# mLSTM heads with the output gate's copy ahead of the strip sums and the denominators behind the next scores; the fourth output unit in a place of its own

## The reference, cut to what matters

```
proj = xn @ w_in                       # q, k (conv + silu), v, o_pre, gates
# each of 8 heads, L x L with causal mask:
dmat = b[t] - b[s] + ig[s];  w_intra = exp(dmat - m_t)
sm   = w_intra * (q @ k.T)             # q, k: 64 wide
num  = sm @ v                          # v: 128 wide
den  = sum(sm, axis=-1)
h    = num / max(abs(den), exp(-m_t))
h    = h * rsqrt(mean(h * h) + eps) * head_gain
out  = (h * sigmoid(o_pre)) @ w_out
# attention, last lines:  o @ w_out, 8 heads of 128
```

## Time and profile before

| | |
|---|---|
| Median of three runs | 2618.55 us |
| Profiled execution, its own time | 2618.54 us |
| Its span | 2616.8 us |
| TensorE matmul busy | 2484.6 us, 95% |
| VectorE busy | 1505.2 us, 58% |
| ScalarE busy | 500.7 us, 19% |
| POOL busy | 1668.6 us, 64% |
| Convolutions and values | about 1940 to 2024 us |
| mLSTM heads | about 2018 to 2197 us |

### The profile page before, as it was taken

How to read it: one execution, slowest core, us unless ns; L and a number is a source line. 1 busy time by engine, 2 the same in 40 slices (tenths; PEclk the granted TensorE clock), 3 DMA queues, 4 the chain that set the end, 5 groups by cost and what they waited for, 6 DMA issues and landing times.

```text
span 2616.8 us, 33925 instructions
## 1 busy us (share of the span) xinstructions
PE 2484.6 (95%) x11933; PEld 2010.5 (77%) x11933; DVE 1505.2 (58%) x1805; ACT 500.7 (19%) x969; POOL 1668.6 (64%) x716
## 2 busy tenths in 40 slices
PE   6998999999999998999999999999999998999998
PEld 4776776777878876888888878888887656887886
DVE  5867324686474467645444565534688667644456
ACT  4533222103000003111111220000131432100000
POOL 4425444577777776565556657877777214777774
PEclk8999999999999998999999999999999878999999
DMA  6212333422332322222222223322322101332331
GB/s 243 73 56 82 117 148 127 157 73 74 99 101 89 108 80 65 85 77 77 84 76 82 82 65 98 108 83 96 105 84 89 33 25 48 96 108 85 93 110 54
DMA packets 61728, 237.86 MB, mean 91 GB/s; under 512 B 7152, under 2 KB 12280, under 8 KB 58048
## 3 DMA queue, kind: packets, MB, share of 16 engines
q1 hardware_dynamic: 55008, 231.56, 26.7%
q10 hardware_dynamic: 6624, 5.03, 0.7%
HBM read 232.37 MB, written 2.10 MB: 90 GB/s over the span
## 4 chain that ended last, share of the span: by engine, by line
PE 81%; DVE 10%; ACT 3%; issue 2%; DVEq 1%; ACTq 1%; POOL 1%; DMA 1%; POOLq 0%
PE gg L575 18%; PE gg L576 18%; PE gg L577 18%; PE babcd L613 2%; PE babcd L614 2%; PE babcd L615 2%; PE gg L958 2%; PE gg L959 1%; PE gg L960 1%; PE babcd L575 1%; PE babcd L577 1%; PE babcd L576 1%; PE be L934 1%; PE babcd L943 1%; DVE tb L2016 1%
## 5 line engine op out<-in xcount | busy, mean ns | idle before, releaser
L475 POOL TENSOR_TENSOR w_hi<-raw,zero 128x1024 fp32r<-128x1024 f32 (+2 forms) x260 | 540.4, 2079 | 457.7 <-PE gg L577 345.4
L477 POOL TENSOR_TENSOR w_lo<-raw,w_hi 128x1024 fp32r<-128x1024 f32 (+2 forms) x260 | 696.2, 2678 | 37.0
L575 PE MATMUL gg<-h_hi,w_hi 128*128 128x512 f32 x1560 | 620.6, 398 | 13.0 <-DVE bf L2398 7.4
L576 PE MATMUL gg<-h_lo,w_hi 128*128 128x512 f32 x1560 | 614.2, 394 | 0.0
L577 PE MATMUL gg<-h_hi,w_lo 128*128 128x512 f32 x1560 | 613.9, 394 | 0.0
L575 PEld LDWEIGHTS gg<-h_hi,w_hi 128*128 128x128 f32 x1560 | 297.4, 191 | 83.5 <-DVE bf L2398 9.8
L577 PEld LDWEIGHTS gg<-h_hi,w_lo 128*128 128x128 f32 x1560 | 296.9, 190 | 63.3
L576 PEld LDWEIGHTS gg<-h_lo,w_hi 128*128 128x128 f32 x1560 | 297.7, 191 | 60.8
L466 POOL TENSOR_TENSOR w_hi<-raw,zero 128x1024 fp32r<-128x1024 f32 (+2 forms) x64 | 140.4, 2193 | 296.7 <-PE babcd L577 152.1
L2115 DVE TENSOR_TENSOR ta<-ff_s,gg 128x512 f32<-128x512 f32 x63 | 43.3, 688 | 320.6 <-PE gg L577 320.6
L575 PE MATMUL gg<-u_hi,w_hi 128*128 128x512 f32 x528 | 209.7, 397 | 4.2 <-issue 4.2
(11 more groups left out here) (623 smaller groups left out, 3960.5 us busy)
## 6 DMA issues: line engine op xcount, KB each, us to landing
raw<-in_w_ff_in_a SPq DMA_DIRECT2D x66, 512.0 KB, 3.5
raw<-in_w_ff_in_b SPq DMA_DIRECT2D x66, 512.0 KB, 3.5
raw<-in_w_att_qk SPq DMA_DIRECT2D x48, 512.0 KB, 3.5
raw<-in_w_ff_out_a SPq DMA_DIRECT2D x24, 704.0 KB, 4.1
raw<-in_w_ff_out_b SPq DMA_DIRECT2D x24, 704.0 KB, 4.1
late_raw<-in_w_ada SPq DMA_DIRECT2D x16, 1024.0 KB, 5.0
raw<-in_w_ml SPq DMA_DIRECT2D x25, 512.0 KB, 3.5
raw<-in_w_merge_a SPq DMA_DIRECT2D x16, 768.0 KB, 5.5
```

The source lines that it names most:

```text
L475: pool.tensor_tensor(hi, a, zero[:].to_broadcast([P, size * P]), ALU.add)
L477: pool.tensor_tensor(lo, a, hi, ALU.subtract).then_inc(S["units_split"], 1)
L575: pe.matmul(dst, w_hi[slot][:, blk], xs[0][:, k, :], start=k == 0, stop=False)
L576: pe.matmul(dst, w_hi[slot][:, blk], xs[1][:, k, :], start=False, stop=False)
```

## The change

In the heads, VectorE copies the output gate right after the products and sums the strips after that; `head_low` follows. TensorE does `head_sums(i-1)` after the first three score blocks of head i, and the scores and weights wait for four of the five `ml_sm` counts of the head before. ScalarE takes `head_deviation(i-1)` ahead of `denominator(i)`. In the convolutions `gate_rows` moves from behind conv(2) to behind conv(3), and `values_out(0)` from ahead of `conv_act(4)` to ahead of `conv_act(3)`. The fourth unit of `w_att_out` and `w_ml_out` is split into the last two tiles of `h_hi` and `h_lo`, free at that time, as soon as all units of the run before have been used.

```diff
+FOURTH = 6
...
+        w_hi.append(h_hi[:, 6:8, :].rearrange("p a b -> p (a b)"))
+        w_lo.append(h_lo[:, 6:8, :].rearrange("p a b -> p (a b)"))
...
-            def split_third(name, tenant, done):
-                u, w = FIRST[name] + 2, THIRD[name]
+            def split_apart(u, w, tenant, done):
                 pool.wait_ge(S[f"raw_landed{u % N_RAW}"], (u // N_RAW + 1) * 16)
                 pool.wait_ge(S[tenant], done)
-                a, hi, lo = raw[u % N_RAW][:, 0:KD * P], w_hi[w][:], w_lo[w][:]
+                a, hi, lo = raw[u % N_RAW][:, 0:KD * P], w_hi[w][:, 0:KD * P], w_lo[w][:, 0:KD * P]
...
                             elif name == "w_att_out":
-                                split_third(name, "att_scores", 14)
+                                split_apart(u0 + 2, THIRD[name], "att_scores", 14)
                             else:
-                                split_third(name, "ml_scores", 4)
+                                split_apart(u0 + 2, THIRD[name], "ml_scores", 4)
+                        elif s == 3 and name in ("w_att_out", "w_ml_out"):
+                            split_apart(u0 + 3, FOURTH, "units_used", u0)
...
-                        cols_mm(g[(u0 + s) % 2], (u0 + s) % 2, kb, xs, ...)
+                        slot = FOURTH if lead is not None and isinstance(i, int) else (u0 + s) % 2
+                        cols_mm(g[(u0 + s) % 2], slot, kb, xs, ...)
...   TensorE, head_scores(i)
-                wait(pe, "ml_sm", 5 * i)
+                wait(pe, "ml_sm", 5 * i - 1)
...
                 for j in (0, 1, 3):
                     block(j)
+                if i:
+                    head_sums(i - 1)
...
                 if i < 7:
                     head_rows(i + 1)
-                head_sums(i)
+            head_sums(7)
...   ScalarE
             for n in range(8):
-                if n == 4:
+                if n == 3:
                     wait(act, "rows_ready", 4)
...   head_weights(i)
-                wait(act, "ml_sm", 5 * i)
+                wait(act, "ml_sm", 5 * i - 1)
...
-                denominator(i)
                 if i:
                     head_deviation(i - 1)
+                denominator(i)
...   VectorE
-                if n == 2:
+                if n == 3:
                     gate_rows()
...   end of head_products(i)
                 v.drain()
+            def strip_sums():
                 own = lambda j: sm_t[:, ML_AT[j]:ML_AT[j] + SEQ - j * P]
                 tt(sm_sum[:], own(0)[:, P:SEQ], own(1), ALU.add)
...
                 head_products(i)
+                output_gate(i)
+                strip_sums()
                 if i > 2:
                     head_low(i - 3)
-                output_gate(i)
                 if i > 1:
                     head_norm(i - 2)
```

More of the change, by code:

```diff
@@ L538, in _ @@
                             if name in ("w_ff0_in_a", "w_att"):
-                                split_third(name, "units_used", u0)
+                                split_apart(u0 + 2, THIRD[name], "units_used", u0)
                             elif name == "w_att_out":
-                                split_third(name, "att_scores", 14)
+                                split_apart(u0 + 2, THIRD[name], "att_scores", 14)
                             else:
-                                split_third(name, "ml_scores", 4)
+                                split_apart(u0 + 2, THIRD[name], "ml_scores", 4)
+                        elif s == 3 and name in ("w_att_out", "w_ml_out"):
+                            split_apart(u0 + 3, FOURTH, "units_used", u0)
                         else:
@@ L680, in pair @@
                         wait(pe, "res_added", i * 2 + (nth * 8 + s - 1))
-                        cols_mm(g[(u0 + s) % 2], (u0 + s) % 2, kb, xs, **(first if isinstance(i, int) and s == 0 else {}))
+                        slot = FOURTH if lead is not None and isinstance(i, int) else (u0 + s) % 2
+                        cols_mm(g[(u0 + s) % 2], slot, kb, xs, **(first if isinstance(i, int) and s == 0 else {}))
                     if shift and isinstance(i, int):
```

## The result

The kernel after takes 2586.56 us, the median of four runs (2585.45 to 2593.54), against 2616.42 us for the kernel before on the same chip: a ratio of 0.989, interval 0.9865 to 0.9915. The profiled executions took 2618.54 (span 2616.8) and 2585.99 us (span 2584.2).

A forecast was written before the change was run, and what follows sets the result against it. TensorE was busy 95% of the span, so only its waits and slow-clock time could move the end. Terms -17.0 - 1.0 - 3.0 + 4.3 - 1.1 + 2.1 = -15.7 took 2618.55 to 2603 us; range 2594 to 2611, 8 in 10.

The forecast's parts named there:

- Heads 2 to 6: mLSTM heads: gate-copy waits of 9.7 us go and slow clock shrinks, 20.7 to 17.3 us each: -17.0, ends -9.7 and -22.
- First head: Head 1: the copy of gate 0 no longer stands behind sums that POOL held up: -1.0 us.
- Convolutions and values: Convolution stage: TensorE's waits of 2.7 and 1.3 us go, second-half values scaled earlier: -3.0, ends 0 and -4.
- Head 7's rows to the first w_ml_out matmul: Last mLSTM head: POOL's consecutive splits block three strip sums and later VectorE operations: +4.3 us, ends -3.1 and +6.
- Fourth w_ml_out unit: w_ml_out: the 4.2 us wait for POOL goes, but VectorE's read of unit 1 limits it: -1.1, ends 0 and -4.2.
- Last attention head: POOL's earlier fourth split blocks two of VectorE's small a_st operations, delaying scaling and transposes: +3.2 us.
- Fourth w_att_out unit: w_att_out: the same gain as for the fourth w_ml_out unit, -1.1 us.
- the short kind: Heads 2 to 6: without stops, most heads would keep only short 1.2 GHz stretches, giving 17.3 us per head.
- VectorE's own loop: Heads: VectorE's sequence of operations per head as the next bound, 16.3 us, behind the low end of -22.
- Rival (b): Heads: the clock stays up, VectorE's loop sets 16.3 us per head, the tail costs little: -25, 2594 us; chance 0.12.
- the strip sums, 4.7 us: Heads: strip sums start 0.9 us after the gate unit's end, POOL's w_hi and w_lo blocking the first and second.
- The denominator: ScalarE in the heads: the deviation goes ahead, leaving one 1.28 us table load before the weights; costs 0 while covered.

The follow-up runs named there:

- gate_dev: Kernel before with the gate copy ahead of the strip sums and the deviation ahead of the denominator, head_sums still ahead of the scores: 2608.27 us, ratio 0.9978.
- gate_sums: Kernel before with the gate copy ahead of the strip sums and head_sums behind the next scores, deviation where it was: 2599.91 us, ratio 0.9943.
- heads_only: Kernel before with all the heads' edits, without those of the convolutions and fourth units: 2578.88 us, ratio 0.9864.
- fourth_late: heads_only plus the fourth units, their splits held back until the last heads' small operations (att_factors, head_squared) are issued: 2576.21 us, ratio 0.9854.

## Why the prediction was wrong

| Term | Predicted | Between the two traces |
|---|---|---|
| Heads 2 to 6 | -17.0 | -30.7 |
| Head 1's rows to head 2's | 0 | -2.1 |
| First head | -1.0 | -1.1 |
| Convolutions and values | -3.0 | +3.9 |
| Head 7's rows to the first w_ml_out matmul | +4.3 | 0.0 |
| Fourth w_ml_out unit | -1.1 | +0.7 |
| Last attention head | +3.2 | +4.4 |
| Fourth w_att_out unit | -1.1 | -0.8 |
| Code not touched (most of it attention) | 0 | -6.9 |
| Sum | -15.7 | -32.6 |

**What failed is the heads' term**, in the step "without the stops I expect the short kind in most heads. I take 17.3 per head". Part of the mechanism was right: the copy goes first, its stop is gone, the clock rises. And "all fast it would be about 14.3" was a good price of a head, since the five heads took 14.6 each. But 17.3 keeps 3.0 us a head for slow clock, some 6 us of it, and the heads after had 3 us of it in all five. The idle time gave 7.5 us for 9.7 predicted, but the clock gave 23.2 for 7.3. My argument that the short kind would stay rested on one window, 2094 to 2100.5, and on two heads with a wait of 0.4 us. Each of them came behind heads that had stopped, so they said little about a TensorE that never stops. The earlier trace rows held the needed bound in another form: a window over all five heads at 0.77 says 48 us of slow clock, and a price of up to 24 us, where my low end for this term was -22.

The bound of that low end, "16.3 is VectorE's own loop", was too high as well. (Its terms add up to 16.5.) Rival (b), at 0.12, is what happened: the clock stays up and this loop sets the pace. But the loop takes 13.8 to 15.7 us, so (b) ended at 2594 where 2586.56 was measured. The term that was too large is the strip sums, 4.7 us, of which I had POOL hold up two in every head. I took the sums to start 0.9 us after the unit's end. In the head shown they start 2.6 us after (2093.78 against 2091.18), because the products are the last to come, and by then POOL is in its second split, which ends at 2095.57 with only the first sum beside it. Of the heads 2 to 6, three have one sum held up and two have none. The Trainium skill (SBUF — State Buffer, SBUF: two separate sides) has the two engines exclude each other for a whole instruction; the 2.20 us for 0.86 and the 0.42 behind it agree with that, and the error was in which instruction meets which.

**The denominator** came as worked out: one table load of 1.28 us between it and the weights, and nothing lost. But its worth was missed. I wrote that moving `head_sums` "adds and removes no instruction" and buys cover. gate_dev and gate_sums show that without one of the two moves 21 to 29 us of the 36 are not there.

**The convolutions** have the wrong sign. "TensorE's 2.7 and 1.3 us go" held, and a wait of 6.4 us took their place. I said that VectorE had as much work as before; it had 7 us more, since `gate_columns` now runs beside POOL's splits and lasts 14.7 us for 7.4. I had looked for this effect in the heads and in attention, and not here.

**The tail.** The late strip sums came (3.89 us of wait for 3.1 before), and the late start of w_ml_out came (an idle 0.9 us). Still the stretch up to w_ml_out is as long as before, 22.57 us, where 2.8 us more were forecast. At the square sums of head 7, where the +4.3 was worked out, it was +1.4 (33.03 us from head 7's rows for 31.60). Two strip sums were held up and not three. The clock gave the rest back: before, 7.3 us right behind the rows were at 0.53, and after, TensorE is at 1.00 from 2124.06 until its stop at 2139.8. (From 2143.66 to 2153.03, behind the stop, it is at 0.52.) The early split is what costs here: heads_only and fourth_late take 21.1 us for the stretch, 1.5 less than before and than after.

**The fourth units.** Both stop for VectorE's read of unit 1, as said: 3.4 us for 4.2. For w_ml_out the gain of 0.8 is lost again before the unit starts. For w_att_out the fourth split came where it was expected, and it held up two operations, as expected, though of 128x32 and 128x16 and not of 128x8. The price, 4.4 us, was not far from the 3.2 forecast, but it came another way, and that is luck. VectorE's factors were 2.7 us later. But ScalarE had scaled the first part by 1507.1, and the transposes came at 1509.27, when TensorE was through with other work: it had stopped 1.6 us longer and then lost 2.6 us at the low clock.

**The rest.** 6.3 of the 6.9 us come before the scores of attention head 7, in code that the change doesn't touch. Both kernels' runs spread over 8 us, and in the fourteen traces these scores start between 1492.3 and 1500.0 us, whatever was edited behind them. So this is how two executions differ. Without it the change is worth some 26 to 30 us, in line with the medians' 29.9. The parts by experiment agree: -36.1 for the heads, +3.1, +5.2, together 2587.2 against 2586.56 measured.

## What to carry to other kernels

Where the granted clock over a stage is under 1.00, work out from it how long TensorE was at 1.2 GHz in the whole stage: half of that is the most that removing the last stop can give, beside the stop itself, and a move that only exchanges one stop for another gave 10 of 36 us here. Judge such edits together, since 10 us and -4 us made 36. Before moving small VectorE operations or a POOL split, look at which of them will then run side by side, in every stage that the move touches.

## What the hardware showed that I had not expected

In the odd heads, whose queries and keys lie in partitions 64 to 127, the score matmuls start 0.01 us after the first matmul of `head_rows`, which uses partitions 0 to 39, and run beside it; in the even heads they follow one another. It is so in all eight heads but the first, whose rows stand elsewhere; that the partitions are the reason is my reading. From the rows to `head_sums` it takes 1.93 us in the odd head (first fence) and 2.41 in the even one:

```profile
2066.47 0.49 PE L1201 MATMUL babcd<-g_r,sel 40*128 40x512 f32 x1
2066.48 0.69 PE L1211 MATMUL babcd<-ml_qk 64*128 64x512 f32 x1
...
2068.40 0.49 PE L1249 MATMUL bf<-sm_t,ones 128*128 128x128 f32 x2
```

```profile
2051.26 0.50 PE L1201 MATMUL babcd<-g_r,sel 40*128 40x512 f32 x1
...
2053.67 0.79 PE L1249 MATMUL bf<-sm_t,ones 128*128 128x128 f32 x2
```

And an operation of 8x128, 0.28 us alone, takes up to 2.5 us beside a POOL split of 128x1024: what it pays is the other's length and not a share of its own.
